# Row averages and three norm sums as pairs of float32r products, in a three-layer forward pass on one core

## The reference

```python
def rms_norm(x, g):
    y = x32 * lax.rsqrt(jnp.mean(x32 * x32, axis=-1, keepdims=True) + NORM_EPS)
    return y.astype(x.dtype) * g

# sparse attention branch of a hybrid layer: 4 heads of 128 for q and for k
q = apply_rope(rms_norm(qc.reshape(b, t, SA_HEADS, SA_HEAD_DIM), q_norm), cos_a, sin_a)
k = apply_rope(rms_norm(kc.reshape(b, t, SA_HEADS, SA_HEAD_DIM), k_norm), cos_a, sin_a)
# delta-rule branch: a triangular system of 128x128 blocks per head is solved
# each layer: h = rms_norm(x, norm_g), then one wide product h @ w_in
```

## Time and profile before

| | us |
|---|---|
| median of 3 runs (1946.12 to 1949.91) | 1947.81 |
| the profiled execution | 1946.41 |
| its span in the trace | 1944.6 |
| TensorE busy | 1930.8 (99%) |
| VectorE busy | 1018.0 (52%) |
| ScalarE busy | 888.2 (46%) |
| POOL busy | 850.2 (44%) |

### The profile page before, as it was taken

How to read it: one execution, slowest core, us unless ns; L and a number is a source line. 1 busy time by engine, 2 the same in 40 slices (tenths; PEclk the granted TensorE clock), 3 DMA queues, 4 the chain that set the end, 5 groups by cost and what they waited for, 6 DMA issues and landing times.

```text
span 1944.6 us, 23731 instructions
## 1 busy us (share of the span) xinstructions
PE 1930.8 (99%) x9106; PEld 1532.8 (79%) x9106; DVE 1018.0 (52%) x1832; ACT 888.2 (46%) x1355; POOL 850.2 (44%) x644
## 2 busy tenths in 40 slices
PE   9999999999999999999999999999999999999999
PEld 6878887877788878787877888677766788888887
DVE  5757755555745668766464647575644436101210
ACT  6455553344345455543344355586555344312321
POOL 5545432433445454422434445455322445444443
PEclk9999999999999999999999999999999999999999
DMA  5334542423535235632414545322111332222232
GB/s 202 128 118 131 138 134 80 155 77 124 185 102 177 88 114 148 163 106 71 153 65 141 192 151 163 135 77 98 65 55 55 119 108 87 99 97 98 98 114 71
DMA packets 94575, 227.69 MB, mean 117 GB/s; under 512 B 29976, under 2 KB 33048, under 8 KB 93152
## 3 DMA queue, kind: packets, MB, share of 16 engines
q1 hardware_dynamic: 88768, 223.03, 35.1%
q10 hardware_dynamic: 5696, 3.15, 0.6%
HBM read 194.01 MB, written 24.64 MB: 112 GB/s over the span
## 4 chain that ended last, share of the span: by engine, by line
PE 86%; DVE 7%; DMA 2%; ACT 2%; SPq 1%; issue 1%; POOL 1%; ACTq 0%; DVEq 0%
PE bank L442 85%; DVE kv L376 1%; DVE ER L376 1%; PE bank L446 1%; SPq L371 1%; DMA X<-inverses 1%; DVE scs L401 1%; DMA kv<-blocks 1%; DVE tmp L376 1%; DVE m8s L398 0%; ACT lt L428 0%; DVE lt L386 0%; DVE tmp L386 0%; ACT wh L431 0%; DMA st<-units 0%
## 5 line engine op out<-in xcount | busy, mean ns | idle before, releaser
L376 POOL TENSOR_TENSOR wl<-st,wh 128x512 fp32r<-128x512 f32 x602 | 803.4, 1357 | 1020.2 <-ACT wh L431 1020.1
L442 PE MATMUL bank<-hh,wh 128*128 128x512 f32 x1616 | 651.2, 404 | 1.9 <-ACT hh L428 0.6
L442 PE MATMUL bank<-hh,wl 128*128 128x512 f32 x1616 | 629.2, 390 | 0.0
L442 PE MATMUL bank<-hl,wh 128*128 128x512 f32 x1616 | 628.8, 390 | 0.0
L431 ACT ACTIVATE wh<-st 128x1024 fp32r<-128x1024 f32 (+1 forms) x302 | 316.8, 1049 | 238.3 <-PE bank L442 190.5
L442 PEld LDWEIGHTS bank<-hh,wh 128*128 128x128 f32 x1616 | 303.3, 188 | 90.5 <-issue 26.0
L442 PEld LDWEIGHTS bank<-hl,wh 128*128 128x128 f32 x1616 | 303.6, 188 | 67.2 <-issue 6.9
L442 PEld LDWEIGHTS bank<-hh,wl 128*128 128x128 f32 x1616 | 303.3, 188 | 64.6
L376 DVE TENSOR_TENSOR xt<-xt,bank 128x512 f32<-128x512 f32 x40 | 27.4, 686 | 236.0 <-PE bank L442 236.0
L428 ACT ACTIVATE tmp<-bank 128x512 f32<-128x512 f32 x70 | 41.7, 596 | 158.2 <-PE bank L442 151.5
L442 PE MATMUL bank<-fh,wh 128*128 128x512 f32 x256 | 99.6, 389 | 0.0
(11 more groups left out here) (344 smaller groups left out, 2833.4 us busy)
## 6 DMA issues: line engine op xcount, KB each, us to landing
st<-units SPq DMA_DIRECT2D x300, 512.0 KB, 3.5
gates<-tmp SPq DMA_DIRECT2D x48, 256.0 KB, 2.7
gt<-gates SPq DMA_DIRECT2D x48, 256.0 KB, 3.6
pads<-tmp SPq DMA_DIRECT2D x32, 128.0 KB, 2.7
qk<-tmp SPq DMA_DIRECT2D x16, 256.0 KB, 4.2
x_scratch<-xt SPq DMA_DIRECT2D x2, 2048.0 KB, 8.7
xt<-x_scratch SPq DMA_DIRECT2D x2, 2048.0 KB, 8.2
ph<-phi SPq DMA_DIRECT2D x8, 512.0 KB, 4.7
```

The lines of the kernel that those rows point to most:

```text
L376: return NOTHING if self.e is None else self.e.tensor_tensor(out, a, b, op)
L442: return NOTHING if self.e is None else self.e.matmul(out, lhsT, rhs, start=start, stop=stop, skip_group_check=share)
```

## The change

The averages of the rows and the norm sums 0, A and B are computed as two float32r products, of exact constants (`onesr`, `meanr`) with a high and a low part of what is summed. The constants are made on VectorE at the start and leave the loaded table. For the rows ScalarE squares a second time, into the float32r tile `sqh`, and POOL subtracts it from the float32 squares into `sql`. The pair of products, ScalarE's root behind it, VectorE's end of the row and SyncE's spill move to later half units. For the norm sums ScalarE copies `nacc` and VectorE subtracts. In `proj2` the `v2` units become jobs of the same `lagged` line. Norm "in" and the sums of q2 and k2 stay float32 products.

```diff
+    onesr, meanr, blkr = [sb(n, [128, 128], F32R) for n in ("onesr", "meanr", "blkr")]
+    tmpr = [sb(f"tmpr{i}", [128, T], F32R, stack=tms) for i in range(2)]
+        L.sqh, L.sql = [sb(f"{n}{l}", [128, T], F32R, stack=dtmp) for n in ("sqh", "sql")]
...
+        def summed(out, exact, high, low):
+
+            pe.mm(out, exact, high, True, False)
+            return pe.mm(out, exact, low, False, True)
...
         def norm(w, frees):
             def total():
-                pe.wait_ge(*at("consts"))
-                pe.wait_ge(*at("nacc", w, 7))
-                pe.mm(bank(7, "norm", w), ones, nacc[:], True, True).then_inc(*sig("norm_mm", w))
+                pe.wait_ge(*at("exact"))
+                if w == "in":
+                    pe.wait_ge(*at("nacc", w, 7))
+                    pe.mm(bank(7, "norm", w), ones, nacc[:], True, True).then_inc(*sig("norm_mm", w))
+                else:
+                    pe.wait_ge(*at("sum_lo", w))
+                    summed(bank(7, "norm", w), onesr[:], tmpr[0][:], tmpr[1][:]).then_inc(*sig("norm_mm", w))
...
             def row(c):
-                yield
-                pe.wait_ge(*at("qk_sq", l, c))
-                pe.mm(bank(3, "qk_mean", l, c), mean, row_tiles(c)[2][:], True, True).then_inc(*sig("qk_mean", l, c))
+                yield from idle(4)
+                pe.wait_ge(*at("qk_lo", l, c))
+                summed(bank(3, "qk_mean", l, c), meanr[:], layer[l].sqh[:], layer[l].sql[:]).then_inc(*sig("qk_mean", l, c))
...
+            def tokens(j):
...
+                    if b == 2:
+                        yield
...
+                for j in range(3):
+                    yield tokens(j), idle(1)
...
@@ scalar norm
+            if w != "in":
+                ac.wait_ge(*at("nacc", w, 7))
+                ac.cp(tmpr[0][:], nacc[:]).then_inc(*sig("sum_hi", w))
...
@@ scalar row
                 ac.act(x2[:], x[:], ACT.Square).then_inc(*sig("qk_sq", l, c))
-                yield
+                if c > 0:
+                    ac.wait_ge(*at("qk_mean", l, c - 1))
+                ac.act(layer[l].sqh[:], x[:], ACT.Square).then_inc(*sig("qk_hi", l, c))
+                yield from idle(4)
                 ac.wait_ge(*at("qk_mean", l, c))
...
@@ vector norm
+            if w != "in":
+                dv.wait_ge(*at("sum_hi", w))
+                dv.tt(tmpr[1][:], nacc[:], tmpr[0][:].bitcast(F32), ALU.subtract).then_inc(*sig("sum_lo", w))
...
@@ vector row
-                dv.wait_ge(*at("qk_sq", l, c))
+                dv.wait_ge(*at("qk_hi", l, c))
...
-                yield
+                yield from idle(4)
                 dv.wait_ge(*at("qk_n", l, c, 1))
...
@@ vector, at the start
+        zero = pad[1]
+        dv.wait_ge(*at("warm"))
+        dv.ts(onesr[:], zero[:, 0:128], 1.0, ALU.add)
+        dv.ts(meanr[:], zero[:, 0:128], 1.0 / 128.0, ALU.add)
...
+        t.then_inc(*sig("exact"))
...
@@ pool
+            def row(c):
+                x2 = row_tiles(c)[2]
+                yield
+                gp.wait_ge(*at("qk_hi", l, c))
+                gp.tt(layer[l].sql[:], x2[:], layer[l].sqh[:].bitcast(F32), ALU.subtract).then_inc(*sig("qk_lo", l, c))
+                yield
...
-                for _ in range(30):
+                for c in range(2):
                     yield tile(), idle(1)
+                for kind, i in rows_and_gates():
+                    yield tile(), row(i) if kind == "row" else idle(1)
...
@@ sync row
-                yield from idle(7)
+                yield from idle(9)
                 sp.wait_ge(*at("qk_o", l, c))
                 sp.dma(qk_d[:, c, :], row_tiles(c)[0][:]).then_inc(*dma(f"spill{c % 2}", "qk", l, c))
```

More of the change, by code:

```diff
@@ L171, in constants @@
     c.add("ident", np.eye(128))
-    c.add("ones", np.ones((128, 128)))
-    c.add("mean", np.full((128, 128), 1.0 / 128.0))
     c.add("first", np.broadcast_to(i[:, None] % 32 == 0, (128, 128)))
-    c.add("blk", (i[:, None] // 64 == i[None, :] // 64))
     c.add("decay", np.where(i[:, None] <= i[None, :], 0.0, NEG))
@@ L292 @@
     "act_heads": "dn_sq dn_r on_sq on_r egl gexp h_eg h_dt h_vb h_xt",
-    "act_rows": "pl_p qk_sq qk_r q2_sq q2_r k2_sq k2_r conv_0 conv2_0 conv_th zc_a pl_a ga_a gelu_a rec_a",
+    "act_rows": "sum_hi qk_hi pl_p qk_sq qk_r q2_sq q2_r k2_sq k2_r conv_0 conv2_0 conv_th zc_a pl_a ga_a gelu_a rec_a",
     "act_attend": "sel_r sp_e ns_e cm_e gs_a",
@@ L296 @@
     "pool_zero": "vcz0 sC0",
-    "dve_small": "colx identr rw0 hb2 small_v hn gcol lam kz0 gs",
+    "dve_small": "exact colx identr rw0 hb2 small_v hn gcol lam kz0 gs",
     "dve_heads": "h_e h_n h_k vn0 sc_e inv",
-    "dve_rows": "qi ki qk_n qk_o q2_n q2r k2_n k2r rope conv_v conv2 gelu rec_v",
+    "dve_rows": "sum_lo qi ki qk_n qk_o q2_n q2r k2_n k2r rope conv_v conv2 gelu rec_v",
     "dve_attend": "top sel sp_r sp_n ns_r ns_n cm_v cm_n",
@@ L534, in build @@
     hh, hl = sb("hh", [128, 8, T], F32R), sb("hl", [128, 8, T], F32R)
+    tms = ExitStack()
+    tmpr = [sb(f"tmpr{i}", [128, T], F32R, stack=tms) for i in range(2)]
+    tms.close()
     tmp = [sb(f"tmp{i}", [128, T]) for i in range(4)]
@@ L700, in K @@
         return col[rows, names[name][0] + i:names[name][0] + i + 1]
-    ident, ones, mean, blk, eps = C("ident"), C("ones"), C("mean"), C("blk"), C("eps")
+    ident, eps = C("ident"), C("eps")
+    ones, blk = onesr[:].bitcast(F32), blkr[:].bitcast(F32)
     first = C("first")
@@ L1151, in proj2 @@
                 for b in range(4):
+                    if j == 0:
+                        bank(b, "vt", b)
+                    if b == 2:
+                        yield
                     o = banks[b][:, 0:280]
@@ L1160, in proj2, with jobs @@
                 t.then_inc(*sig("unit", n))
-                yield
+            def jobs():
+                for j in range(4):
+                    yield (tile(("c2", (512, 640, 768, 1024)[j]), 6 + j % 2, (("kv", "k2")[j // 2], j % 2), "nA"),
+                           both(query(j), idle(1) if j < 2 else key(j - 2)))
+                for j in range(3):
+                    yield tokens(j), idle(1)
+            yield from lagged(jobs())
         def compress():
@@ L2681, in vector_program @@
         dv.set(pad[1][:], 0.0).then_inc(*sig("warm"))
+        zero = pad[1]
+        dv.wait_ge(*at("warm"))
+        dv.ts(onesr[:], zero[:, 0:128], 1.0, ALU.add)
+        dv.ts(meanr[:], zero[:, 0:128], 1.0 / 128.0, ALU.add)
+        for g, r in enumerate(G2):
+            for f, c in enumerate(G2):
+                t = dv.ts(blkr[r, c], zero[r, c], float(f == g), ALU.add)
+        t.then_inc(*sig("exact"))
         dv.wait_ge(*at("norm_col"))
```

## The result

The changed kernel takes 1985.39 us (median of 4 runs, 1983.28 to 1989.09) against 1948.03 for the kernel before on the same chip (4 runs): 1.0198 times, 95% interval 1.0186 to 1.0211. I had forecast 1963 and a range of 1950 to 1974. The sign is right; the size, 15 more than before, is less than half of the 37 that came.

What follows compares the result with a forecast made beforehand. TensorE, busy 99% of the span, was taken as the bound. Two layers at +9.2 (+18.4), norm sums -1.2 and v2 -0.5 gave +16.7 on 1946.41, about 1963 us; range 1950 to 1974.

Steps and rivals of the forecast that it cites:

- just hidden: Gate's bank behind ScalarE's root and Tanh: free at 5.3, wanted at 5.9, two turns after the pair, so no cost.
- Pair instead of f32 product: Average and norm sums on TensorE: two float32r products cost 0.45 against 0.87, gaining 0.41 us per site.
- Norm sums and v2: Three norm sums as pairs save 1.2 us; reordered v2 products fill idle time before the last k2 sum, saving 0.5.
- Side work "hidden": Second Square on ScalarE and POOL subtraction per row: done 7.1 after the tile's end, product due at 10.9, so no cost.
- Bank 3: Row averages meeting index scores in banks 2 and 3: new stalls 0.8 (turn 11), 1.8 (turn 47); old meetings save 0.3, 0.5.
- Row 4's copy: ScalarE's copy of row 4 waits about 4 us for row 2's spill; TensorE loses 0 to 0.5.
- Turn 11: Half unit 11, Y's Exp behind root and Tanh: further stall 2.5; head 3's products net +1.7, bounds -1.6 to +2.7.
- End 230.75+1.7-2.2-(0 to 1.9): VectorE's block inverse in layer 0: starts 1.7 later, sheds row 3's and row 2's operations, ends 228.4 to 230.3, taken 229.4.
- The spill: Main term: row 3 ends behind the inverse, delaying its spill, row 5's copy and the first X product to 254.5: +8.7 a layer.
- The clock rival: Long TensorE stalls followed by stretches at 1.2 GHz: +11 to +22 us, 1974 to 1985; chance 0.07.
- The gain is kept: Rival: row 3's spill lands before bank 0 is wanted (234.3), about -10, 1937.5 or 1941; chance 0.15.
- chain half hidden: Rival: spill lands at 235 and the inverse's transposed trip shrinks, +2 to +4 a layer, 1946 to 1951; chance 0.09.

Runs made afterwards that it cites:

- row 1's root behind: Changed kernel with row 1's root one turn later on ScalarE, behind gate 8's Tanh and the weight split: 1984.06 us.
- sums and v2 alone: Changed kernel with its rows exactly as before, keeping only the three norm sums as pairs, the v2 order and constants made on chip: 1944.94 us, 0.9994 times before.
- place alone: Kernel before with only its f32 average, root, VectorE's row end and row spill placed as late as in the change: 1980.06 us, 1.0173 times before.
- high squares only: Changed kernel without POOL's subtraction and the second product, so row averages use only the high squares: 1979.76 us.
- the side work: Norm sums and v2 as changed, rows in old places, plus second Square and an unused same-size POOL subtraction: 1949.81 us, 1.0015 times before.
- rows 0 and 1 even and row 3 ahead: Changed kernel with rows 0 and 1 three half units behind, not four, and row 3's VectorE end and spill in their old turns: 1964.21 us.

## Why the prediction was right in direction and short in size

The steps that failed both set the time at which the inverse ends: the root ahead of the Tanh, which I had called "just hidden", and the length of the inverse, which I had only made shorter. The chain behind the inverse held.

- **Pair instead of f32 product: right.** At norm B the pair starts at 1640.71 and the next product at 1641.17: 0.46, forecast 0.45. Norm sums and v2: -1.5 measured alone, -1.7 forecast.
- **Side work "hidden": wrong.** I costed the Square and the subtraction at nothing; alone they cost 4.9 (about 2 to 7). They do not stand on the path of the product, but in front of ScalarE's and POOL's weight splits, and POOL's operations hold VectorE's. Which of the two makes the 4.9 no run separates.
- **Bank 3: right place, smaller.** Forecast stalls 0.8 and 1.8, measured 0.38 (turn 11) and 1.22 (turn 47). Row 4's copy, for which I had 0 to 0.5, costs 1.23 at 221.68.
- **Turn 11: within the bound but for the clock.** Head 3's products came at 170.72 instead of 166.27, +4.45; I had +1.7 and an upper bound of 2.7. In it are 0.92 at `wi`, 0.38 at bank 3, 0.44 at `ER`, 1.00 at `lT`, and a stretch at the lower level of the clock from 157.4 to 160.8 (512 columns 0.43 from one to the next instead of 0.23), 1.6 together. The run with row 1's root behind, the same in order up to here, has the waits and not the stretch: +2.6. I had not seen that row 0's average gave `wi` its time in turn 8, and had no term for the clock.
- **"The gate's bank is free at 5.3 and wanted at 5.9: just hidden": the step that failed.** It prices the root ahead of the Tanh only at the bank. I had named SyncE's waits for the row's spill, and not the gate's spill, which sits in the same odd turn ahead of the block transfers, nor the weight split behind the root. In turn 17 that holds the inverse's data: with head 3's products 4.45 late, the start is 8.2 late (190.88 for 182.64), so the held queue adds 3.8, which I had at nothing; one turn's shift of one root takes 4.5 off the same distance.
- **"End 230.75+1.7-2.2-(0 to 1.9)": wrong by 11.6, and this is the term in which the failed step lands.** The start gives 6.5 of that (8.2 for 1.7): 3.8 from the held queue, 2.7 from head 3's products. The rest, 5.1, is the length, a second step that failed: I took row 3's 2.2 and up to 1.9 of row 2 out of 48.1, so 44.0 to 45.9, and got 50.2, with the stretched part 5.4 larger. So the subtraction was right and the assumption that the operations keep their lengths was wrong; a shift of VectorE's queue against POOL's was not in my list of unknowns.
- **The spill: mechanism right, size nearly right.** 23.6 from the end of the inverse to the X product for 25.1 forecast, and 15.0 before. Taken from the run with the sums and v2 alone, the 19.6 at the X product are 10.3 of later start, 0.9 of length and 8.4 of round trip. I had called the spill the main term; it is the smaller part. Behind the X product a layer loses 1.5 more (the `v` products at 413.63 for 393.31, less 18.8), forecast 0.5.
- **The clock rival happened in small.** Seven products at 0.43 after the 10.5 stall, the stretch from 157.4 to 160.8, much the same in layer 1, and eight behind a wait near 1266: some 3 a layer and 1.6 there, not the 5.5 to 11 a layer of the rival. The measured 1985 lies at the end of that rival's 1974 to 1985, but that is luck: the clock makes about 8 of the 42.9. The chance of 0.07 treated it as a case apart; it is an additional term of any long stall and belongs into the forecast itself. The Trainium skill (TensorE: Matmul & The Clock Gate, What's actually happening) has an idle array drop to the lower clock, and after the stalls of 10.5 the trace agrees. The stretch at 157.4 has no such stall before it, only the waits of 0.44 and 1.00.
- **Outside the layers.** Between 1241 and 1272 the profiled execution loses another 4.0 against the run with the sums and v2 alone: a wait of 2.14 for VectorE's `lt` and the slow products behind it. Such a wait is in six of the nine profiles of kernels with pairs (1.4 to 2.7) and in that of the side work, and not in those of before, sums and v2 alone, place alone or high squares only. Why is open.
- **The sum.** 40.0 in the layers, 4.0 here, -1.5 of sums and v2: 42.5 of the span's 42.9. "The gain is kept" and "chain half hidden" are out.

What stays open is how much of the loss the alignment of VectorE with POOL makes by itself, and how the 19 us divide that the run with rows 0 and 1 even and row 3 ahead still has above the sums and v2 alone. In it are the end of the inverse, 6.4 later with an inverse 5 longer, the 3.84 at row 5's low squares with thirteen slow products behind, and in its profiled execution (1968.29, the slowest of four) some 9 us of lower clock in all.

## What to carry to other kernels

When a step is moved in programs that are ordered by hand, list for every engine what stands behind it in the new turn, and follow each of these through all queues to the end, the transfers of another chain above all; the bank or buffer of the step's own work is only one of them. A cost of the form "it waits a little and is hidden" has to be checked at each in-order queue that it holds, here ScalarE, then SyncE and POOL. Take a product's saving only where no late work hangs on it: sixteen pairs everywhere made this kernel 2% slower, and four in quiet places cost it nothing.

## What the runs showed of the hardware

- VectorE's operations with two SBUF inputs and POOL's subtractions advance one by one: an operation of 0.34 takes 1.31 beside a POOL operation, and one of 0.69 (`tmp<-tmp,nacc` at 217.10 in the changed kernel) takes 1.67. It is a toll per operation, so short ones suffer most. An operation with one input in PSUM pays nothing: `ER<-bank,tpc,cst` takes 0.34 beside POOL and without it.
- After a stall the products run at the lower level (1.2 GHz, 0.43 apart) for a while that does not grow with the stall: 7 products after 10.5 us, 11 after 8.7, 9 after 5.0, 13 after 3.5. In the changed kernel the level was low from 242.8 to 253.0, while the stall ended at 249.98: part of the slow time falls into the stall. Stalls of 1.2 were followed by none at 221.68 in the changed kernel, and by seven near 282.4 in the run with rows 0 and 1 even. A stall of 3.5 cost 6.1 in this way.
- Row 3's spill, a DMA of 256 KB, took 4.8 from issue to landing in the changed kernel, where the forecast took the 4.0 of the earlier trace rows. Such spills scatter: the four between 186 and 262 in the kernel before took 2.1 to 5.6.
